# Hybrid decoder step on one Trainium2 core: query inverse roots applied to rows of scores

## The reference

```python
qa = (_partial_rope(_rmsnorm(qa.reshape(ha), a_q_norm), pos) * A_SCALE).reshape(g5)
ka = _partial_rope(_rmsnorm(ka.reshape(ha), a_k_norm), pos).reshape(g5)
...
s = jnp.einsum('nbqhe,nbkhe->nbhqk', qb, kb, preferred_element_type=jnp.float32)
...
s = jnp.where(mask[None, :, None], s, NEG)
lse = jax.nn.logsumexp(s, axis=-1)
p = jnp.exp(s - lse[..., None])
o = jnp.einsum('nbhqk,nbkhe->nbqhe', p, vb.astype(jnp.float32))
```

## Time and profile before

| | |
|---|---|
| median of 3 runs | 875.22 us (874.59 to 875.29) |
| profiled execution | 874.67 us |
| its span (first to last instruction) | 872.8 us |
| PE busy | 868.2 us |
| DVE busy | 618.0 us |
| ACT busy | 479.9 us |
| POOL busy | 188.4 us |
| granted TensorE clock | 1.000 |

### The profile page before, as it was taken

The page is one execution under the profiler, slowest core; times in us unless marked ns, Lnnn a source line. Parts: engine busy times, 40 slices in busy tenths (PEclk is TensorE's granted clock), DMA queues, the critical chain, the costliest instruction groups (busy, mean ns, idle before and its releaser), DMA issues.

```text
span 872.8 us, 19244 instructions
## 1 busy us (share of the span) xinstructions
PE 868.2 (99%) x7848; PEld 847.7 (97%) x7848; DVE 618.0 (71%) x934; ACT 479.9 (55%) x762; POOL 188.4 (22%) x211
## 2 busy tenths in 40 slices
PE   9999999999999999999999999999999999999998
PEld 8999999999999999999999999989899999999998
DVE  6766665567687688888888869986469676666453
ACT  7443443456545587776776567555646544443432
POOL 0433331000000000019986006000010133332000
PEclk9999999999999999999999999999999999999999
DMA  9999878999998888999998998798899799989771
GB/s 337 404 350 312 306 260 308 341 361 390 343 320 283 299 307 321 338 356 377 416 406 269 349 356 299 283 343 308 329 341 354 268 390 382 378 311 325 225 199 38
DMA packets 63399, 281.14 MB, mean 322 GB/s; under 512 B 8264, under 2 KB 9416, under 8 KB 61712
## 3 DMA queue, kind: packets, MB, share of 16 engines
q1 hardware_dynamic: 24144, 148.31, 44.0%
q10 hardware_dynamic: 39168, 131.61, 43.9%
HBM read 256.64 MB, written 111.32 MB: 422 GB/s over the span
## 4 chain that ended last, share of the span: by engine, by line
PE 98%; DVE 1%; DMA 0%; issue 0%; ACT 0%; ACTq 0%
PE acc L468 17%; PE acc L469 16%; PE acc L470 16%; PE att L468 12%; PE att L469 11%; PE att L470 11%; PE aux L1208 2%; PE att L1261 1%; PE aux L1172 1%; PE att L846 1%; PE aux L1519 1%; PE att L521 1%; PE att L1303 1%; DMA raw<-w 0%; PE att L1000 0%; PE att L999 0%
## 5 line engine op out<-in xcount | busy, mean ns | idle before, releaser
L448 DVE TENSOR_TENSOR wl<-raw,wh 128x1024 fp32r<-128x1024 f32 (+2 forms) x278 | 331.5, 1193 | 168.9 <-ACT wh L442 164.1
L442 ACT ACTIVATE wh<-raw 128x1024 fp32r<-128x1024 f32 (+2 forms) x278 | 275.4, 995 | 186.7 <-PE att L470 94.1
L468 PE MATMUL acc<-hh,wh 128*128 128x264 f32 x496 | 144.8, 292 | 0.1
L470 PE MATMUL acc<-hh,wl 128*128 128x264 f32 x496 | 141.0, 284 | 0.0
L469 PE MATMUL acc<-hl,wh 128*128 128x264 f32 x496 | 140.8, 284 | 0.0
L468 PE MATMUL att<-xh,wh 128*128 128x264 f32 x392 | 111.6, 285 | 0.0
L469 PE MATMUL att<-xl,wh 128*128 128x264 f32 x392 | 111.2, 284 | 0.0
L470 PE MATMUL att<-xh,wl 128*128 128x264 f32 x392 | 111.2, 284 | 0.0
L468 PE MATMUL acc<-xh,wh 128*128 128x264 f32 x384 | 109.3, 285 | 0.0
L470 PE MATMUL acc<-xh,wl 128*128 128x264 f32 x384 | 108.9, 284 | 0.0
L469 PE MATMUL acc<-xl,wh 128*128 128x264 f32 x384 | 108.9, 284 | 0.0
(11 more groups left out here) (318 smaller groups left out, 2094.4 us busy)
## 6 DMA issues: line engine op xcount, KB each, us to landing
raw<-w ACTq DMA_DIRECT2D x206, 512.0 KB, 7.7
state<-state_in SPq DMA_DIRECT2D x32, 512.0 KB, 9.8
state_out<-state SPq DMA_DIRECT2D x32, 512.0 KB, 8.4
raw<-w ACTq DMA_DIRECT2D x32, 384.0 KB, 5.4
kv<-cache SPq DMA_DIRECT2D x24, 512.0 KB, 7.3
raw<-w ACTq DMA_DIRECT2D x32, 320.0 KB, 5.4
raw<-w SPq DMA_DIRECT2D x8, 512.0 KB, 9.2
kv_out<-cache SPq DMA_DIRECT2D x3, 960.0 KB, 7.9
```

The source lines that it names most:

```text
L442: nc.scalar.activation(wh[n % HI_RING][:, 0:slot_size(n)], raw[n % RAW_RING][:, 0:slot_size(n)], ACT.Copy).then_inc(hi_done, 1)
L448: nc.vector.tensor_tensor(wl[n % RAW_RING][:, 0:slot_size(n)], raw[n % RAW_RING][:, 0:slot_size(n)], wh[n % HI_RING][:, 0:slot_size(n)].bi ...
L468: nc.tensor.matmul(out, w_hi, xh, start=first, stop=False)
L470: return nc.tensor.matmul(out, w_lo, xh, start=False, stop=last)
```

## The change

The queries of the prompt stay unscaled in `qk`. Their inverse roots reach the scores instead: in slot 18 TensorE transposes the 32 rows of roots in four small matmuls (`pe_q_roots`), VectorE copies the result (`dve_q_roots`) to `q_roots` (a column for each head, a row for each query of a half), and `dve_scores` multiplies each row of scores by its root while it adds the mask. As the three groups of a head slot have different roots, this takes three instructions (256, 64 and 64 columns); the row maximum is an instruction of its own. Only the keys are still spread, in slots 28 to 33. Besides: the state outputs of slots 24 to 31 are made in slots 28 and 32 instead of 26, 28, 30 and 32; single v tiles stand at step 3 instead of 1; gate B's sigmoid stands ahead of the split of `ob`; VectorE's `att_sum` (second inverse of a block) stands ahead of the decode steps; both `act_prob` of a block stand together, ahead of the high half.

```diff
-        def act_qk_rhi(act, which):
+        def act_qk_rows(act, which):
             act.wait_ge(qk_rinv_done, which + 1)
             if which:
-                act.wait_ge(qk_spread, AT // 2 * which)
+                act.wait_ge(qk_spread, 1)
             for e in range(4):
...
+        def pe_q_roots(pe):
+
+            pe.wait_ge(qk_rows, 4)
+            for qb in range(2):
+                for s in range(2):
+                    last = nc.tensor.matmul(bank4[s * AE:(s + 1) * AE, 32 * qb:32 * qb + 32], qk_rinv[0:32, qb + 2 * s:S:CLASSES],
+                                            ident[0:32, 0:32], start=True, stop=True)
+            last.then_inc(qk_spread, 1)
+
+        def dve_q_roots(dve):
+            dve.wait_ge(qk_spread, 1)
+            nc.vector.tensor_copy(q_roots[:], bank4[:, 0:64].rearrange("p (q n) -> p q n", q=2)).then_inc(qk_done, 1)
...
-            nc.vector.tensor_tensor_reduce(prob[r][:], att4[:, r, 0:3 * P], const("mask")[:, S * qb:S * qb + 3 * P], 1.0, LOWEST,
-                                           ALU.add, ALU.max, att_m[:, r, 0:1]).then_inc(att_masked, 1)
-            dve.wait_ge(att_masked, n + 1)
+            wide, narrow = P * qb, S - S * qb
+            for g, cols in enumerate((slice(wide, wide + S), slice(narrow, narrow + AE), slice(narrow + AE, narrow + P))):
+                head_at = 2 * (4 * g + i // 2) + r
+                masked = nc.vector.scalar_tensor_tensor(prob[r][:, cols], att4[:, r, cols], q_roots[:, qb, head_at:head_at + 1],
+                                                        const("mask")[:, S * qb + cols.start:S * qb + cols.stop], ALU.mult, ALU.add)
+            masked.then_inc(att_masked, 1)
+            dve.wait_ge(att_masked, 2 * n + 1)
+            nc.vector.tensor_reduce(att_m[:, r, 0:1], prob[r][:], AX.X, ALU.max).then_inc(att_masked, 1)
+            dve.wait_ge(att_masked, 2 * n + 2)
...
-        SPREAD_AT = {18 + u: u for u in range(AT // 2)}
-        SPREAD_AT.update({28 + u: AT // 2 + u for u in range(AT // 2)})
+        SPREAD_AT = {28 + u: u for u in range(AT // 2)}
+        ROOTS_AT = 18
         PAIR_STEP = 6
-        STATE_TURN = {s: [slot for slot in range(s - 4, s) if slot in STATE_SLOT] for s in range(4, 2 * AT + 1, 4)}
-        STATE_TURN.update({s: [slot for slot in (s - 2, s - 1) if slot in STATE_SLOT] for s in range(2 * AT + 2, 3 * AT - 3, 2)})
+        STATE_TURN = {s: [slot for slot in range(s - 4, s) if slot in STATE_SLOT] for s in range(4, 3 * AT - 3, 4)}
...
+                act.wait_ge(pe_half, 4 * p_gb.q0 + t + 1)
+                nc.scalar.activation(gate_b[:, t], acc[bank_of(p_gb, t)][:, 0:T], ACT.Sigmoid).then_inc(out_of["act"], 1)
                 if 2 <= t < 2 + RH:
                     split_ob(t - 2)
-                act.wait_ge(pe_half, 4 * p_gb.q0 + t + 1)
-                nc.scalar.activation(gate_b[:, t], acc[bank_of(p_gb, t)][:, 0:T], ACT.Sigmoid).then_inc(out_of["act"], 1)
...
-                if second:
-                    if i < ATT:
-                        act_prob(act, i, 1)
-                else:
+                if not second:
...
                         act_prob(act, i, 0)
+                        act_prob(act, i, 1)
...
                 att(i)
+                att_sum(i)
                 dec_steps(i)
                 if i in DEC_OUT:
                     dve_dec_out(dve, DEC_OUT[i])
-                att_sum(i)
...
                 if t in V_TURNED:
-                    steps[PAIR_STEP if 2 * AT + t in STATE_TURN else 1].append(lambda: v_tile(V_TURNED[t]))
+                    steps[PAIR_STEP if 2 * AT + t in STATE_TURN else 3].append(lambda: v_tile(V_TURNED[t]))
```

More of the change, by code:

```diff
@@ L200, in trunk_step @@
         pick = fixed("pick", [B], F32R)
+        q_roots = fixed("q_roots", [2, 32])
         sq_s, rinv_s = square_sum[:, 0:2 * AT * B], rms[:, 0:2 * AT * B]
@@ L1053, in act_qk_rms @@
             act.wait_ge(qk_ms_psum, AT * (which + 1))
-            if which:
-                act.wait_ge(qk_rlo, which)
             nc.scalar.activation(qk_rinv4[:], bank5[:, which * S:which * S + AE], ACT.Sqrt, bias=eps,
@@ L1061, in dve_qk_rinv, with act_qk_rhi, dve_qk_rlo @@
             nc.vector.reciprocal(qk_rinv4[:], qk_rinv4[:]).then_inc(qk_rinv_done, 1)
-        def act_qk_rhi(act, which):
+        def act_qk_rows(act, which):
             act.wait_ge(qk_rinv_done, which + 1)
             if which:
-                act.wait_ge(qk_spread, AT // 2 * which)
+                act.wait_ge(qk_spread, 1)
             for e in range(4):
                 nc.scalar.activation(qk_rinv[0:32, e * AE:(e + 1) * AE], qk_rinv4[32 * e:32 * e + 32], ACT.Copy).then_inc(qk_rows, 1)
-            act.wait_ge(qk_rows, 4 * which + 4)
+        def pe_q_roots(pe):
[8 more added lines that the diff above has]
+            nc.vector.tensor_copy(q_roots[:], bank4[:, 0:64].rearrange("p (q n) -> p q n", q=2)).then_inc(qk_done, 1)
+        def act_qk_rhi(act):
+            act.wait_ge(qk_rows, 8)
             nc.scalar.activation(qk_rhl[0:32], qk_rinv[0:32], ACT.Copy).then_inc(qk_rhi, 1)
-        def dve_qk_rlo(dve, which):
-            dve.wait_ge(qk_rhi, which + 1)
+        def dve_qk_rlo(dve):
+            dve.wait_ge(qk_rhi, 1)
             nc.vector.tensor_tensor(qk_rhl[32:64], qk_rinv[0:32], qk_rhl[0:32].bitcast(F32),
@@ L1117, in pe_qk_spread @@
         def pe_qk_spread(pe, u):
-            pe.wait_ge(qk_rlo, 2 * u // AT + 1)
-            if u:
-                pe.wait_ge(qk_done, u)
+            pe.wait_ge(qk_rlo, 1)
+            pe.wait_ge(qk_done, u + 1)
             for n in range(2):
-                i = (2 * u + n) % AT
+                i = 2 * u + n
                 last = nc.tensor.matmul(bank4[:, n * S:(n + 1) * S], sel[:, i * P:(i + 1) * P], qk_rhl[:], start=True, stop=True)
@@ L1127, in dve_qk_norm @@
         def dve_qk_norm(dve, u):
-            dve.wait_ge(qk_spread, u + 1)
-            dve.wait_ge(qk_turned, 2 * u + 2)
-            two = qk[:, 2 * u:2 * u + 2, 0:S]
+            dve.wait_ge(qk_spread, u + 2)
+            dve.wait_ge(qk_turned, AT + 2 * u + 2)
+            two = qk[:, AT + 2 * u:AT + 2 * u + 2, 0:S]
             nc.vector.tensor_tensor(two, two, bank4[:].rearrange("p (n t) -> p n t", n=2), ALU.mult).then_inc(qk_done, 1)
@@ L1247, in pe_scores @@
             if i:
-                pe.wait_ge(att_masked, 2 * i)
+                pe.wait_ge(att_masked, 4 * i - 1)
             else:
@@ L1677, in _ @@
                 if n == STATES - 4:
-                    sp.wait_ge(qk_rhi, 2)
+                    sp.wait_ge(qk_rhi, 1)
                     sp.wait_ge(ret_stored, 16 * RH)
@@ L1682, in _ @@
             roll_more(sp, 2)
-            sp.wait_ge(qk_done, AT)
+            sp.wait_ge(qk_done, AT // 2 + 1)
             for i in range(1, 5):
@@ L1831, in qk_quad @@
                     if t == AT + 4:
-                        act_qk_rhi(act, 0)
+                        act_qk_rows(act, 0)
                     act_ahead(act, p_qk.q0 + qq, j)
@@ L1846, in _ @@
                 if t == 2:
-                    act_qk_rhi(act, 1)
+                    act_qk_rows(act, 1)
+                    act_qk_rhi(act)
                 if t in V_TURNED:
@@ L2026, in qk_slot @@
                     dve_qk_rinv(dve, s // (2 * AT))
-                if s in (AT + 4, 2 * AT + 3):
-                    dve_qk_rlo(dve, s // (2 * AT))
+                if s == ROOTS_AT:
+                    dve_q_roots(dve)
+                if s == 2 * AT + 3:
+                    dve_qk_rlo(dve)
                 if s == 2 * AT + 3:
@@ L2124, in _ @@
                 att(16 + t)
+                att_sum(16 + t)
                 dec_steps(16 + t)
@@ L2268, in slot_steps @@
                     steps[1].append(lambda: pe_qk_samples(pe))
+                if s == ROOTS_AT:
+                    steps[4].append(lambda: pe_q_roots(pe))
                 if s in SPREAD_AT:
@@ L2295, in small_sum @@
                 pe.wait_ge(small_step, 1)
-                pe.wait_ge(qk_done, AT)
+                pe.wait_ge(qk_done, AT // 2 + 1)
                 nc.tensor.matmul(bank4[:, 0:RH * B], ones, os_sum[:].rearrange("p h b -> p (h b)"), start=True,
```

2 lines of the change are left out of this document (removed).

## The result

The changed kernel takes 887.95 us (median of 5 runs, 887.53 to 890.29), the kernel before 874.63 us (5 runs, 874.58 to 875.29): the ratio is 1.0152, 95% interval 1.0141 to 1.0163. It is 13.3 us slower, where the forecast was 9.0 us slower; 887.95 lies inside the range of 876 to 888 us by 0.05 us, and outside the forecast's own range of 881 to 887. The sign was right, and so were four of the seven places where waits were forecast; the size was not.

A forecast was written before the change was run, and what follows sets the result against it. TensorE's instruction stream was taken to bound the kernel (busy 868.2 of 872.8 us). New waits of 10.9 us less 1.9 us of stream gave +9.0 us, 884.2 us; own range 881 to 887, widened to 876 to 888.

The forecast's parts named there:

- The stream, 1.9 us less: TensorE's instruction stream: removed pairs 1.4, transposes -0.5, regrouped state outputs 0.4, v tile 0.3, sigmoid 0.3 us; 1.9 us less.
- rival D: State 31's late load holds ScalarE: 1 to 2 us on top, 885.5 us; chance 0.03 with anything worse.
- VectorE's row half, 1.63 us: VectorE's `dve_scores` with its negative maximum per row half: 1.63 us instead of 0.72, bounds 1.20 to 1.85.
- rival A: No semaphore wait costs VectorE anything: row half 1.39 us, waits 7.0, time 880.3 us; chance 0.15 including what lies towards C.
- Block 1: TensorE waits for ScalarE's `prob` ahead of the turns of attention block 1: 2.6 us.
- Gather 0: TensorE waits at the first gather, whose own rows come late behind `act_prob` and the high and low halves: 2.4 us.
- Decode turn: TensorE waits on VectorE at turn 1 of decode, slot 17: 2.5 us.
- Gate A: TensorE waits for gate A's tanh of slot 18, forecast 1.82 + 0.51 us later: 1.2 us.
- Blocks 2, 3, 4: TensorE waits ahead of the turns of attention blocks 2, 3 and 4: 0.6, 0.1 and 1.5 us.
- The slope, 0.8 us for 0.05 us a row half: By the same layout, TensorE's summed waits change some 0.8 us for each 0.05 us of VectorE's row half cost.
- B: VectorE's added work is hidden and TensorE only loses its 1.9 us: 873.3 us, faster; chance 0.12.
- C: VectorE catches up between blocks; only gather and decode turn cost, 2 to 3 us: 874.5 to 876.5 us; chance 0.08.

The follow-up runs named there:

- filled_short: The changed kernel with 8 filler matmuls on TensorE ahead of each of its three waits of 2.3 us; 884.77 us, ratio 1.0114.
- one_piece: The changed kernel with one scalar_tensor_tensor over 384 columns of a row half instead of three, leaving out two groups' roots; 883.11 us, ratio 1.0096.
- roots_early3: The changed kernel with VectorE's order made anew and gate A's tanh of tiles 0 and 2 moved on ScalarE, same arithmetic; 873.76 us, 0.9989 of the kernel before.
- roots_early: The changed kernel with VectorE's order made anew and gate A's tanh of tile 2 moved on ScalarE, same arithmetic; 877.01 us, ratio 1.0025.
- forced_waits: The kernel before, with TensorE made to wait for GpSimd clears at five halves of the q and k projections; 893.86 us, ratio 1.0212.
- roots_old_order: The changed kernel with both new orders undone, VectorE's second inverse and ScalarE's second act_prob; 881.56 us, ratio 1.0073.
- hold_gather: The kernel before, with TensorE made to wait for GpSimd clears at gather 0 and the decode turn of slot 17; 877.49 us, ratio 1.0041.

## Why the prediction was right in sign and place, and short in size

- *The stream, 1.9 us less.* Right: 2.0 us. The transposes of `pe_q_roots` hold the stream for 0.59 us, 0.10 more ahead of them and 0.11 more behind them, 0.8 (forecast 0.5, bounds 0.4 to 1.2); six pairs 6 x 0.25 = 1.5 (forecast 1.4); the regrouping and the v tiles together 1.0 instead of 0.7; the sigmoid 0.3 as forecast. The regrouping's late load (rival D) never held ScalarE: the load was issued at 483.09, and the state was scaled at 494.17 with no idle time ahead of it.
- *VectorE's row half, 1.63 us.* 1.55. The reduction, which waits for its predecessor, starts 0.03 us after its end (565.14 against 564.25 + 0.86), and the next row half, which doesn't, 0.08 before the end of the negative maximum (565.80 against 565.73 + 0.15), as in the earlier trace rows; rival A, for which the Trainium skill ("VectorE: DVE Perf Modes", section "The DRAIN you can't avoid") spoke, gave 1.39 for it. The measured value is nearer to the row's.
- *The exposed wait of the second inverse, 0.64 us a block.* 0.70 us.
- *Waits one by one.* Block 1: 2.25 us (2.6). Gather 0: 2.26 (2.4). Decode turn: 2.29 (2.5). Gate A: 1.12 (1.2). Blocks 2, 3, 4: none over 0.3 us (0.6, 0.1, 1.5). Sum 7.9 instead of 10.9 us: the lateness of VectorE was forecast within 0.4 us at each of the four places, and the three other terms came to nothing. Block 4's wait appears in filled_short (0.74 us), once TensorE isn't slowed ahead of it.
- *The step that failed* is the heading of the layout, "clock of before": TensorE was taken to run at 2.4 GHz behind its waits. The traces show 6.8 us lost at 1.2 GHz, in three stretches, and 0.6 us in restarts. These 7.4 us, less the 3.0 us by which the waits were put too high, 0.1 us of the stream and 0.6 us by which the base of the forecast (875.22) stood above the median of the runs here (874.63), make the 3.7 us between 884.2 and 887.95. That the two large errors partly cancel, and that the result stays 0.05 us inside the range, is luck.
- *The slope, 0.8 us for 0.05 us a row half.* 0.35 in waits (one_piece; for the time, 4.8 us for 0.24 us, it is 1.0, as the clock comes with the waits). The slope let all seven waits of the layout shrink; those of blocks 2 to 4 weren't there, and gather 0 kept its 2.26 us.
- *Rivals.* B (hidden, 873.3 us) and C (VectorE catches up) were wrong for this order; A (880.3 us) counted one term lower and failed as the forecast did, since it had no clock in it either. But roots_early3 reaches 873.8 us with the same work, so what B needed was another order and no faster VectorE. The two new orders were in the sum (0.64 us a block and 0.51 us), but no rival asked what the change would cost without them: they make 6.7 of the 13.3 us.

What stays open: why the clock falls behind 0.4 and 0.5 us of waiting at gather 0 (filled_short, roots_early) and not behind 2.4 us among big products. At gather 0 TensorE goes on with many small fp32 matmuls, behind forced_waits' third wait with big ones; that this is the reason was not tried. The 0.8 us that the sum of forced_waits leaves over were not traced either, nor why one fall behind gather 0 doesn't show in the times of roots_old_order and filled_short.

## What to carry to other kernels

Where TensorE is the bound, a new wait costs its length and what the clock does behind it: here 7.9 us of waits cost 6.8 us more. Read the granted clock behind each new wait before you explain a time by waits, and expect filling or removing one wait to bring out the next that the slow clock had covered. When a saturated engine gets more work, first ask in what order it takes it: work that others wait for ahead of work with slack (here 5 us and more for the low halves), and independent work in the gap between an instruction and the answer that it needs; the same instructions took 888.0 us in one order and 873.8 in another.

## What was not expected of the hardware

- TensorE's granted clock went from 1.00 to 0.50 in the attention stretch 1.1 to 1.4 us after TensorE had gone on behind waits of 2.25 to 2.29 us, and stayed there for 3.4 to 6.8 us; among big products it stayed at 1.00 behind 2.39 us and fell behind 2.97 us. The Trainium skill ("TensorE: Matmul & The Clock Gate", section "HAM oscillation — how this bites in real kernels") describes a TensorE that waits for data at every step of a loop and goes on at the lower clock each time. The traces agree that waiting lowers the clock; they add that one wait in a stream that is otherwise full is enough, and that behind the three waits of the changed kernel TensorE first went on at 1.00.
- The executions of one kernel with the same held places differ: 876.7 us at 1.000, 878.3 at 0.998 and 879.8 at 0.996 (hold_gather).
- A filler of 128 columns made as an fp32 matmul holds the stream for 0.234 us, while the transposes of the turns, of the same size, take 0.14 each (0.82 us for six).
